# Scores of two heads made together on the two halves of the array's rows, in the dilated attention of a two-block kernel

## What is computed

```python
DILATED_PATTERNS = ((128, 1), (512, 4), (2048, 16))
def dilated_mixture_attention(q, k, v):
    outs, lses = [], []
    for window, dilation in DILATED_PATTERNS:
        o, lse = dilated_window_attention(q, k, v, window, dilation)
        outs.append(o)
        lses.append(lse)
    wts = jax.nn.softmax(jnp.stack(lses, axis=0), axis=0)
    o = jnp.sum(wts[..., None] * jnp.stack(outs, axis=0), axis=0)
    return o.astype(q.dtype)
```

## Time and profile before

| | |
|---|---|
| median of 3 runs | 2346.64 us |
| span of the profiled execution, first to last instruction | 2338.8 us |
| the profiled execution's own time | not listed apart from its span |
| TensorE busy | 2196.2 us, 94% |
| DVE / ACT / GpSimd busy | 1139.8 / 636.7 / 822.2 us |
| attention, first scores to last output matmul | 1278.3 to 1469.1 us, 190.8 us |
| mean granted TensorE clock | 0.980 |

### The profile page before, as it was taken

One profiled execution on the slowest core, in us unless ns is written; L12 is line 12 of the kernel. 1 busy time (PEld: TensorE's weight loads), 2 busy tenths in 40 slices (PEclk: granted clock), 3 DMA queues, 4 the chain that ended last, 5 costly groups with the idle time before them and its releaser, 6 DMA issues.

```text
span 2338.8 us, 26219 instructions
## 1 busy us (share of the span) xinstructions
PE 2196.2 (94%) x10721; PEld 1821.2 (78%) x10721; DVE 1139.8 (49%) x1156; ACT 636.7 (27%) x876; POOL 822.2 (35%) x320
## 2 busy tenths in 40 slices
PE   2999999999999999979999999897999999999998
PEld 2788878888787768857887688776888888878886
DVE  5787688787765446565332666234000000025556
ACT  5333433344411012150203555223000000011212
POOL 2332222322324435424543000142444444445552
PEclk9999999999999999989999899998999999999999
DMA  9111100110111111232111000132111111111122
GB/s 356 32 32 29 35 27 27 33 30 27 36 46 36 45 37 45 80 146 73 43 48 45 1 1 1 42 129 82 45 50 48 45 54 45 45 45 54 46 102 87
DMA packets 129973, 130.31 MB, mean 56 GB/s; under 512 B 6310, under 2 KB 103031, under 8 KB 128888
## 3 DMA queue, kind: packets, MB, share of 16 engines
q1 hardware_dynamic: 123208, 113.08, 15.1%
q10 hardware_dynamic: 6704, 16.36, 1.9%
HBM read 116.84 MB, written 12.58 MB: 55 GB/s over the span
## 4 chain that ended last, share of the span: by engine, by line
PE 81%; DVE 12%; issue 3%; ACT 2%; DMA 1%; ACTq 0%; DVEq 0%
PE psum L394 12%; PE psum L396 12%; PE psum L395 12%; PE psum L414 10%; PE psum L416 9%; PE psum L415 9%; PE psum L521 3%; PE psum L808 3%; PE psum L797 2%; DVE arena L1348 1%; PE psum L787 1%; DVE arena L1399 1%; DVE arena L1369 1%; PE psum L638 1%; DVE arena L1380 1%
## 5 line engine op out<-in xcount | busy, mean ns | idle before, releaser
L372 POOL TENSOR_TENSOR w_hi<-w_raw,ones 128x1024 fp32r<-128x1024 f32 x158 | 388.8, 2461 | 1477.9 <-PE psum L396 813.8
L394 PE MATMUL psum<-h_hi,w_hi 128*128 128x512 f32 x1472 | 585.4, 398 | 1.6 <-POOL w_lo L375 1.1
L396 PE MATMUL psum<-h_hi,w_lo 128*128 128x512 f32 x1472 | 574.3, 390 | 0.0
L395 PE MATMUL psum<-h_lo,w_hi 128*128 128x512 f32 x1472 | 574.2, 390 | 0.0
L375 POOL TENSOR_TENSOR w_lo<-w_raw,w_hi 128x1024 fp32r<-128x1024 f32 x158 | 433.3, 2742 | 12.4
L414 PE MATMUL psum<-w_hi,h_hi 128*128 128x512 f32 x1056 | 412.9, 391 | 16.4 <-DVE h_lo L1542 9.8
L415 PE MATMUL psum<-w_lo,h_hi 128*128 128x512 f32 x1056 | 412.0, 390 | 0.0
L416 PE MATMUL psum<-w_hi,h_lo 128*128 128x512 f32 x1056 | 411.9, 390 | 0.0
L394 PEld LDWEIGHTS psum<-h_hi,w_hi 128*128 128x128 f32 x1472 | 277.5, 188 | 60.1 <-issue 4.3
L396 PEld LDWEIGHTS psum<-h_hi,w_lo 128*128 128x128 f32 x1472 | 277.0, 188 | 58.3
L395 PEld LDWEIGHTS psum<-h_lo,w_hi 128*128 128x128 f32 x1472 | 277.4, 188 | 57.3 <-issue 2.4
(11 more groups left out here) (190 smaller groups left out, 2053.4 us busy)
## 6 DMA issues: line engine op xcount, KB each, us to landing
w_raw<-w_in SPq DMA_DIRECT2D x68, 512.0 KB, 3.8
w_raw<-w_out SPq DMA_DIRECT2D x24, 512.0 KB, 3.5
w_raw<-w_gate SPq DMA_DIRECT2D x22, 512.0 KB, 3.8
w_raw<-w_up SPq DMA_DIRECT2D x22, 512.0 KB, 3.8
w_raw<-w_down SPq DMA_DIRECT2D x22, 512.0 KB, 3.5
arena<-ada_w SPq DMA_DIRECT2D x8, 1024.0 KB, 13.9
x_mid<-arena ACTq DMA_DIRECT2D x16, 512.0 KB, 2.9
arena<-x_mid SPq DMA_DIRECT2D x16, 512.0 KB, 8.0
```

Source lines behind the costliest of these rows:

```text
L372: pool.tensor_tensor(w_hi[:, c, :].rearrange("p (a n) -> p a n", n=P), raw.rearrange("p (a n) -> p a n", n=P), unit_scale, ALU.mult).then_ ...
L394: pe.matmul(o, wh, xh, start=(k == 0), stop=False)
L395: pe.matmul(o, wh, xl, start=False, stop=False)
L396: return pe.matmul(o, wl, xh, start=False, stop=(k == KT - 1))
```

## The change

In PE's list a `qk_pair(m)` stands for `qk(2m)` and `qk(2m + 1)`. It makes the scores of heads `2p` and `2p + 1` of one query block, the even head into slot 0 and the odd head into slot 1, chunk by chunk; within a chunk it alternates: `hi*hi` of the even head, `hi*hi` of the odd, `hi*lo` even, `hi*lo` odd, `lo*hi` even, `lo*hi` odd. It waits once, until `s_moved` is `2m`: until both slots have been read. Then the SGU group, `p_t` and `pv` of both iterations follow, in the old order. The other engines' lists stay as they are.

```diff
-            def qk(n):
-                i, h = n // AH, n % AH
-                if n >= 2:
-                    pe.wait_ge(s_moved, n - 1)
-                po = DH * (h % 2)
-                for c0 in range(0, (i + 1) * P, HALF):
-                    c1 = min(c0 + HALF, (i + 1) * P)
-                    o = two_banks(n % 2)[:, c0:c1]
-                    qh, ql = [x[po:po + DH, h // 2, i * P:(i + 1) * P] for x in (h_hi, h_lo)]
-                    kh, kl = [x[po:po + DH, 4 + h // 2, c0:c1] for x in (h_hi, h_lo)]
-                    pe.matmul(o, qh, kh, start=True, stop=False)
-                    pe.matmul(o, qh, kl, start=False, stop=False)
-                    mm = pe.matmul(o, ql, kh, start=False, stop=True)
-                mm.then_inc(s_full, 1)
+            def qk_pair(m):
+                i, p = 2 * m // AH, m % (AH // 2)
+                if m:
+                    pe.wait_ge(s_moved, 2 * m)
+                w = (i + 1) * P
+                for c0 in range(0, w, HALF):
+                    c1 = min(c0 + HALF, w)
+                    o = [two_banks(e)[:, c0:c1] for e in range(2)]
+                    qh, ql = [[x[DH * e:DH * e + DH, p, i * P:(i + 1) * P] for e in range(2)] for x in (h_hi, h_lo)]
+                    kh, kl = [[x[DH * e:DH * e + DH, 4 + p, c0:c1] for e in range(2)] for x in (h_hi, h_lo)]
+                    for e in range(2):
+                        pe.matmul(o[e], qh[e], kh[e], start=True, stop=False)
+                    for e in range(2):
+                        pe.matmul(o[e], qh[e], kl[e], start=False, stop=False)
+                    for e in range(2):
+                        mm = pe.matmul(o[e], ql[e], kh[e], start=False, stop=True)
+                        if c1 == w:
+                            mm.then_inc(s_full, 1)
...
-            for n in range(N + 3):
-                if n < N:
-                    qk(n)
-                if 0 <= n - N_SGU < SGU_G:
-                    sgu(n - N_SGU)
-                if 0 <= n - 2 < N:
-                    p_t(n - 2)
-                if 0 <= n - 3 < N:
-                    pv(n - 3)
+            for m in range(N // 2 + 2):
+                if m < N // 2:
+                    qk_pair(m)
+                for n in (2 * m, 2 * m + 1):
+                    if 0 <= n - N_SGU < SGU_G:
+                        sgu(n - N_SGU)
+                    if 0 <= n - 2 < N:
+                        p_t(n - 2)
+                    if 0 <= n - 3 < N:
+                        pv(n - 3)
```

## The result

The changed kernel took 2309.84 us, the median of 4 runs between 2308.30 and 2311.31 us, beside 2346.55 us for the kernel before on the same chip: ratio 0.9837, interval 0.9823 to 0.9851, or 35 to 42 us less. On a second chip it was 2308.64 us beside 2343.02 (0.9847, 0.9824 to 0.9869). The forecast was 2317 us with a range from 2309 to 2331: the direction and most of the mechanism were right, and the kernel gained about a quarter more than forecast (36.7 instead of 29.2 us). By the ratio the kernel lies at 0.9837 of the 2346.64 us that the forecast started from, 2308.4 us, just under the range.

A forecast was written before the change was run, and what follows sets the result against it. TensorE was taken to bind the large attention stages, ACT those of 384 and 512 keys. Savings of 22.7 + 3.2 + 3.3 = 29.2 us gave a span of 2309.6 us; plus 7.8, 2317 us, range 2309 to 2331.

The forecast's parts named there:

- Two halves at once: Attention scores: matmuls on different halves of the rows overlap fully, 0.035 us extra a pair; as summed, chance 0.72.
- The passage between 64 and 128 rows: TensorE in the attention: going over between 64-row and 128-row matmuls costs 0.15 us a unit, saved once a pair.
- the rival without overlap: Scores of the two halves don't overlap; only passages are saved, 0.34 us a pair: 2338 us, chance 0.03.
- The lost buffer: A pair waits for both score slots; nothing paid in large stages, 0.9 us charged to the stage of 640 keys.
- Stages of 384 and 512 keys: 1313.8 to 1348.2 us: ACT decides, its idle time bounds the saving; 1.4 + 1.8 = 3.2 us, bounds 1 and 5.8.
- the clock in the stage of 256 keys: Clock rising at the same moment gives 1.2 us back; one step sooner, some 1.5 us more saved.
- from the span to the runs: Whole kernel: the median of the runs lies 7.8 us above the profiled span, added to 2309.6 us.
- Partial overlap: Scores with 512 columns: the halves overlap only in part, 1.3 sets a pair, 9 to 10 us lost: 2327 us, chance 0.11.
- draining at each change of half: Scores: every change of half drains the array, 288 x 0.11 = 32 us: 2370 us, chance 0.03.
- DVE or ACT as the bound up to 640 keys: Units 16 to 39: the lost buffer costs 0.5 to 1 us a pair and the gain there goes: 2325 us, chance 0.07.
- A longer low clock: Start of the attention: clock stays at 0.50 longer; to 1325 us it costs 13 us, 2330 us, chance 0.04.
- the starts in pairs: Sign in the changed profile: score lines in pairs starting within 0.04 us of each other, also with 512 columns.

The follow-up runs named there:

- experiment 2: Changed kernel with both heads of a pair taken from partitions 0 to 63, the same half of the rows: 2337.31 us beside 2346.29 for the kernel before.
- experiment 9: Changed kernel with DVE doing both biases and maxima of a pair before its other work: 2306.78 us beside 2308.64 for the changed kernel.
- experiment 6: Kernel before, no pairs of scores, two SGU products next to each other behind every second unit of 8 to 15: 2340.41 us beside 2341.51.
- Experiments 3 to 5: Kernel before with pairs only in units 16 to 63, only in 0 to 15, or only in 8 to 15: 2318.70, 2336.47 and 2339.19 us.
- experiment 7: Changed kernel with three extra 512-column fp32 matmuls in TensorE's wait ahead of the attention: 2310.15 us beside 2308.64 for the changed kernel.
- experiment 1: Kernel before, profiled and timed once more without edit: 2346.21 us, median of 10 runs from 2338.26 to 2351.04, each span 1.6 us below its time.
- experiment 8: Changed kernel with all matmuls of a pair's even head before all of the odd head: 2320.15 us beside 2308.64 for the changed kernel.
- experiments 3 and 4: Kernel before with pairs only in units 16 to 63 (the late pairs), 2318.70 us, or only in units 0 to 15, 2336.47 us.

## Why the prediction missed, point by point

**Two halves at once: right, and whole.** The step taken from units 0 and 1 at half clock holds for 512 columns at full clock; experiment 2 shows that it is this, and what it is worth (28 us). The 3.07 of 4 in the Trainium skill, "TensorE: Matmul & The Clock Gate", Part 3, is for four row tiles, and the estimate worked out from it, 1.3 sets a pair, did not hold for two halves here: 1.59 us for two heads where one took 1.60.

**The passage between 64 and 128 rows: right in the sum.** Pairs of 1024 keys start 7.06 us apart (1414.23 to 1421.29 us in the profile) against 7.1 forecast and 8.8 before. The 0.34 us a pair in the rival without overlap follows from no row; experiment 2 measured 8.82 - 8.41 = 0.41 us.

**The lost buffer: right.** In the stages of 768 keys and more TensorE is busy all but 0.1 us. The charge of 0.9 us in the stage of 640 keys was somewhat high: that stage saved 4.8 instead of 4.3. By the Trainium skill, "TensorEngine Tiling (Array Packing)", PSUM Bottleneck, the emptying may come to bind: in the smaller stages it does a little (TensorE's 3.6 us of waits for DVE), in those of 768 keys and more not. The waits were not where the prediction had them ("only in units 2 to 7 and 24 to 35"): they stand ahead of units 2, 8, 12, 16, 18, 40, 42 and 44.

**Stages of 384 and 512 keys: ACT's bound right, the clock left out.** The stage of 512 keys saved 0.1 instead of 1.8 us. ACT's chain stands there as forecast:

```profile
1326.45 1.28 ACT L892 ACT_TABLE_LOAD   x1
...
1328.46 1.28 ACT L1188 ACT_TABLE_LOAD   x1
...
1330.48 0.61 ACT L1180 ACTIVATE arena<-arena 128x512 f32<-128x512 f32 x1
...
1332.72 0.58 ACT L882 ACTIVATE arena<-psum 128x512 f32<-128x512 f32 x1
```

From the first table load to the copy for which the next transposes wait it is 6.3 us on ACT alone, with two loads and three squares between, and TensorE waits 2.4 us at its end. But that was so before, too: 6.3 us from 1337.43 to 1343.69, and this wait at its end:

```profile
PE psum L797 <- ACT arena L877: 2.2, 1, 2.2
```

What the profile of before lacks is a stretch at 0.50 near the end of that wait, 3.4 us long after the change. Of the 13 profiles here 11 have one, of 3.4 to 10.2 us, four with single units in this stage among them; the prediction's profile and experiment 9's have the wait and no such stretch. The stage with single units and 3.4 us at 0.50 (experiment 6), and with pairs and none (experiment 9, with its other order on DVE):

```profile
1324.20:1346.10 21.90, 19.71 (x113) 15.24 (x112) 13.88 (x29) 16.47 (x38) 0.00 (x0) 0.92 0.00 1
```

```profile
1320.60:1338.30 17.70, 14.69 (x115) 11.95 (x114) 13.84 (x30) 16.65 (x39) 0.00 (x0) 1.00 0.00 1
```

At the same low clock the pairs save 21.9 - 20.2 = 1.7 us of this stage, the forecast's 1.8. The shortfall against the profile of before is the clock, which fell here in one and not in the other.

**The term that failed: the clock in the stage of 256 keys.** The prediction's step read: "If the clock rises at the same moment, most of that pair is at half clock and gives 1.2 us back", with 1.5 us for a rise one step sooner. It rose 13.6 us sooner, and the stage saved 8.0 us instead of 1.6. Experiments 3 to 5 show that the early rise comes with the pairs and with that stage, and that the pairs of units 0 to 15 are worth 8 to 10 us in the runs; experiment 6, in one profile, that two neighbouring 512-column products alone have most of the same effect on the clock; experiment 7, that idle time ahead isn't what keeps the clock low. I had the sign right ("denser work speaks for an equal or sooner rise") and gave it 1.5 us, where it was 6.4. By the Trainium skill, "TensorE: Matmul & The Clock Gate", Part 1, activity releases the clock; the direction agrees with what is seen here, but TensorE was busy 26.25 of 27.00 us before at 0.50, so its busy share would not have told the moment. Why the clock rises at that point of the work stays open.

**The second term: from the span to the runs.** The sum for the span was 2309.6 and the profile has 2306.7: off by 2.9 us (the attention saved 4.2 us more than forecast, and 1.4 us were lost ahead of it and behind). The time is off by 7.6 from the sum's 2317.4. The other 4.7 us are the 7.8 that I put between span and median, where the changed kernel has 3.1. Of the 7.8, 1.6 lie outside the span (experiment 1), and 6.2 are what this one execution was faster by than the median run of its kernel, for the most part by less 0.50 clock, as far as experiment 1 shows. Both profiles of the changed kernel have the early rise. Why before's runs scatter over 12 to 15 us and the changed kernel's over 1 to 3 is only partly explained: with three matmuls added ahead of the attention (experiment 7) its runs scatter over 7.6 us. What makes the clock fall at a place in one run and not in another stays open.

**Rivals and signs.** Partial overlap, none, and draining at each change of half are ruled out by the timeline. DVE or ACT as the bound up to 640 keys did not take the gain: the stage of 640 keys saved more than forecast, and those of 384 and 512 keys what ACT left, at the same clock. A longer low clock turned out with the opposite sign at the start. Of the signs, the starts in pairs, the 1.6 us and the 7.1 us came as written; the attention took 157.3 instead of 162 us. And the clock was at 0.50 once past 1310 us, a sign of being wrong that the prediction named: not because it had stayed down, but because it fell again for 3.4 us at 1333.

## What to carry to other kernels

Two matmuls of 64 contraction rows whose operands lie in different halves of the partitions and whose results go to different banks cost one, if they stand next to each other in TensorE's list (experiment 8: three matmuls apart they still ran together, six apart not). Two results in one bank were not tried. Before taking that gain, check which stages are TensorE's: what another engine's chain holds, or a table load, gives nothing back. Compare a stage only with one at the same granted clock: the stage of 512 keys seemed to save 0.1 us and saved 1.7. Where a stretch is at half clock, the order of its work can move the moment at which the clock rises (17.1 instead of 27 us or more in experiment 6), which the time of the whole kernel need not show. And take a profile's distance to the median of runs as scatter, here mostly of the clock, and not as a constant.

## What the runs showed of the hardware

- TensorE starts matmuls out of the order of the list when they lie on different halves of the rows, up to three matmuls ahead in what was seen (experiment 8; and units 0 and 1 of before). By the Trainium skill, "TensorE: Matmul & The Clock Gate", Part 3, matmuls start and end strictly in order; the rows here differ, and they decide.
- Two sets of scores on two halves of the rows took 1.59 us, on one half 2.95 us, one set alone 1.60 us (512-column matmuls at full clock).
- The granted clock was at 0.50 while TensorE was busy 10.05 of 10.20 us (experiment 7) and 30.24 of 30.70 (the late pairs of experiments 3 and 4): a busy TensorE is not by itself a fast one.
- One kernel's executions scattered by 0.6%, the slower ones mostly with the lower mean clock. The 9 runs of the changed kernel scattered by 0.1%; that its order of work is the cause isn't shown.
